# Two queue positions moved in a one-core fp32 transformer kernel: a weight split between two copies of transposed attention weights, and the memory's keys and values ahead of two splits

## The reference, cut to what matters

```python
def swiglu(h, wg, wu, wd):
    return (jax.nn.silu(h @ wg) * (h @ wu)) @ wd

def memory_cross_attention(h, mem_n, wq, wk, wv, wo, g_q, g_k):
    ...
    k = rms_norm((mem_n @ wk).reshape(B, M, MEM_HEADS, HEAD_DIM), g_k)
    v = (mem_n @ wv).reshape(B, M, MEM_HEADS, HEAD_DIM)
    ...

def attend(args):
    ...
    p = jax.nn.softmax(sc, axis=-1).astype(v_c.dtype)
    return jnp.einsum('bhqk,bkhd->bqhd', p, v_c)
```

## Time and profile before

| | us |
|---|---|
| median of 3 runs | 1170.08 (1169.73 to 1170.96) |
| the profiled execution | 1169.77 |
| its span in the profile | 1167.9 |
| busy PE / DVE / ACT / POOL | 1155.3 / 890.6 / 600.7 / 54.6 |
| granted clock of PE, mean | 1.00 |

### The profile page before, as it was taken

One profiled execution on the slowest core, in us unless ns is written; L12 is line 12 of the kernel. 1 busy time (PEld: TensorE's weight loads), 2 busy tenths in 40 slices (PEclk: granted clock), 3 DMA queues, 4 the chain that ended last, 5 costly groups with the idle time before them and its releaser, 6 DMA issues.

```text
span 1167.9 us, 15522 instructions
## 1 busy us (share of the span) xinstructions
PE 1155.3 (99%) x5969; PEld 965.9 (83%) x5969; DVE 890.6 (76%) x1598; ACT 600.7 (51%) x797; POOL 54.6 (5%) x109
## 2 busy tenths in 40 slices
PE   9999999999999999999999999999999999999998
PEld 7888888888889988888888887888898787888887
DVE  6666577987857768798886996888568777979874
ACT  7744454544445555454344464444467867545441
POOL 1100010000000000000001300000110002000000
PEclk9999999999999999999999999999999999999999
DMA  7744536555444443665453645465355142555530
GB/s 289 288 154 158 211 113 245 220 216 194 172 176 178 148 145 145 234 234 215 170 192 131 259 176 212 181 233 196 133 208 189 38 145 72 201 232 216 216 144 36
DMA packets 34689, 213.56 MB, mean 183 GB/s; under 512 B 4665, under 2 KB 6841, under 8 KB 10041
## 3 DMA queue, kind: packets, MB, share of 16 engines
q1 hardware_dynamic: 34617, 212.59, 49.0%
HBM read 211.53 MB, written 1.05 MB: 182 GB/s over the span
## 4 chain that ended last, share of the span: by engine, by line
PE 95%; DVE 2%; ACT 1%; DMA 1%; issue 1%; SPq 0%; POOL 0%; DVEq 0%; POOLq 0%
PE ps L325 30%; PE ps L326 29%; PE ps L327 29%; PE ps L331 3%; PE ps L762 1%; DVE wlo L1504 1%; DMA raw<-in_w_v 1%; PE ps L813 1%; PE ps L635 1%; PE ps L790 0%; PE ps L615 0%; DVE tmp L1523 0%; PE ps L737 0%; ACT xThi L1072 0%; PE ps L823 0%
## 5 line engine op out<-in xcount | busy, mean ns | idle before, releaser
L1504 DVE TENSOR_TENSOR wlo<-raw,whi 128x2048 fp32r<-128x2048 f32 (+2 forms) x196 | 433.1, 2232 | 45.1 <-ACT whi L1051 45.1
L1051 ACT ACTIVATE whi<-raw 128x2048 fp32r<-128x2048 f32 (+2 forms) x196 | 364.9, 1868 | 152.4 <-DMA raw<-in_w_gu 80.3
L325 PE MATMUL ps<-whi,xThi 128*128 128x512 f32 (+2 forms) x960 | 373.6, 389 | 4.3 <-issue 2.8
L327 PE MATMUL ps<-whi,xTlo 128*128 128x512 f32 (+2 forms) x960 | 371.0, 386 | 0.0
L326 PE MATMUL ps<-wlo,xThi 128*128 128x512 f32 (+2 forms) x960 | 370.8, 386 | 0.0
L325 PEld LDWEIGHTS ps<-whi,xThi 128*128 128x128 f32 x960 | 180.4, 188 | 42.9 <-issue 4.4
L327 PEld LDWEIGHTS ps<-whi,xTlo 128*128 128x128 f32 x960 | 180.4, 188 | 36.4
L326 PEld LDWEIGHTS ps<-wlo,xThi 128*128 128x128 f32 x960 | 180.5, 188 | 35.0
L1636 DVE STREAM_TRANSPOSE f_sil<-f_hid 32x128 f32<-32x128 f32 x640 | 193.8, 303 | 13.1 <-DVE f_hid L1628 0.9
L325 PE MATMUL ps<-whi,f_hThi 128*128 128x512 f32 x352 | 138.3, 393 | 0.0
L327 PE MATMUL ps<-whi,f_hTlo 128*128 128x512 f32 x352 | 137.3, 390 | 0.0
(11 more groups left out here) (289 smaller groups left out, 1160.9 us busy)
## 6 DMA issues: line engine op xcount, KB each, us to landing
raw<-in_w_gu SPq DMA_DIRECT2D x88, 1024.0 KB, 4.8
raw<-in_w_dn SPq DMA_DIRECT2D x44, 1024.0 KB, 5.2
raw<-in_w_u SPq DMA_DIRECT2D x8, 1024.0 KB, 6.3
raw<-in_w_ao SPq DMA_DIRECT2D x8, 1024.0 KB, 5.2
raw<-in_w_v SPq DMA_DIRECT2D x6, 1024.0 KB, 5.0
raw<-in_w_bv SPq DMA_DIRECT2D x4, 1024.0 KB, 4.9
raw<-in_w_bk SPq DMA_DIRECT2D x4, 1024.0 KB, 4.7
raw<-in_w_bq SPq DMA_DIRECT2D x4, 1024.0 KB, 4.9
```

Of the source, the lines that this page charges most:

```text
L325: e.matmul(ps, a[0], b[0], start=start, stop=False)
L327: return e.matmul(ps, a[1], b[0], start=False, stop=stop)
L1051: e.activation(dst[:, cs], raw_cols(i, cs), ACT.Copy).then_inc(*inc("whi", i, p))
L1504: e.tensor_tensor(lo[:, cs], raw_cols(i, cs), hi[:, cs].bitcast(F32), ALU.subtract).then_inc(*inc("wlo", i, p))
```

## The change

```diff
--- before.py
+++ after.py
@@ -1479,10 +1479,10 @@
         keys = mem_keys()
 
         def beside(c):
+            if c in (2, 3, MEM_CHUNK):
+                next(keys)
             if c == MEM_CHUNK:
                 split(2)
-            if c in (2, 3, MEM_CHUNK):
-                next(keys)
             if c == MEM_CHUNK + 4:
                 e.wait_ge(*at("clamped"))
                 a = ang[:, :, :, :].rearrange("p a b c -> p (a b c)")
@@ -1734,9 +1734,11 @@
                 weights(g)
                 if g < 3:
                     keys(g + 1, "k")
-                if g != 1:
+                if g > 1:
                     split()
                 turned_p(g, 0)
+                if g == 0:
+                    split()
                 turned_p(g, 2)
                 if g < 3:
                     keys(g + 1, "q")
```

## The result

| | us |
|---|---|
| before, median of 9 runs | 1170.08 (1169.25 to 1171.85) |
| changed, median of 9 runs | 1166.25 (1165.85 to 1167.20) |
| ratio, with its 95% interval | 0.9960 (0.9951 to 0.9968) |
| the profiled executions | 1169.77 and 1166.23 |
| their spans | 1167.9 and 1164.4 |

The change makes the kernel faster, by 0.4%. The two profiles differ by 3.54 us, where 3.47 was forecast, and the medians by 3.83. The ratio says more: 4.7 us, and the end of its interval that is nearest to 1 still says 3.7. Two questions follow.

A forecast was written before the change was run, and what follows sets the result against it. PE bounds the kernel, busy 1155.3 of 1167.9 us, leaving 12.6 us to win. Gains of 3.0 (ACT) and 0.46 (DVE), given as 3.47 us, take the median from 1170.08 to 1166.6; range 1165.8 to 1168.0.

The forecast's parts named there:

- That the gap is the copy's: Third FFN, chunk 4: PE's 2.8 us "issue" wait is for ACT's copy to `vm`, queued behind two splits.
- Its length, by starts, 3.0 us: PE's gap before unit pair 124/125, costed from matmul starts: 2.93 + 0.07 = 3.0 us gained by the ACT edit.
- the idle column: Profile's PE idle time, resting on modelled ends: 2.77 us at the `vm` gap, 3.17 us for both edits.
- the sum, 3.47: Both edits together: 3.0 us on ACT plus 0.46 us on DVE, 3.47 us gained.
- The edit on DVE, 0.46 us: Attention, head group 0: head 0's turned-weights copy steps ahead of one split, removing PE's `a_pT` wait; 0.46 us.
- Where the moved splits go: ACT's splits of units 127, 128, 129 begin at 719.4, 721.3, 723.2: later by 3.7, 2.9, 1.0 us.
- leads of 10.9 and 9.1 us: Time between DVE finishing the low halves of units 127 and 128 and PE needing them: 10.9 and 9.1 us.
- 0 for the moved splits: Delaying ACT's splits in the third FFN costs 0, covered by DVE's 7.48 us idle stretch.
- the slower rival: Low halves of units 127 and 128 miss PE's need; 6.6 us lateness falls on PE, 1173.2 us; chance 0.02.
- the step to the median: Whole kernel: profiled execution 1169.77, 0.31 under median 1170.08, becomes 1166.3, so the median becomes 1166.6 us.
- part given back: ACT's third split delays chunk 5's silu; 1.2 us of the gain is lost at later PE waits, 1167.8; chance 0.09.
- the other two: `vm` gap not due to the copy, 1169.6 us, chance 0.05; late low halves slow PE, 1173.2 us, chance 0.02.

The follow-up runs named there:

- the filled kernel: 10 unused identity matmuls added on PE where it waits for `vm`, against the kernel before; median 1170.02 us, ratio 0.9993.

## Why the prediction was right or wrong

*That the gap is the copy's*: right. It went with the ACT edit alone, grew with a third split, and once PE had work in it the profile put its name to it. *Its length, by starts, 3.0 us*: right, 2.94 from P to G (2.98 with the ACT edit alone) and the 0.07 or so of the second matmul's late start. By the Trainium skill's page "Perfetto Trace Analysis", section "Per-engine timelines", TensorE's end times are modelled. The traces agree that the starts are the better reading: 2.94 to 2.98 us went, where the idle column has 2.77. That the sum, 3.47, is so near to the 3.54 of the two profiles is in part luck, since starts of the same kernel differ by some tenths from profile to profile; and its two parts, 3.00 and 0.46, make 3.46.

*The edit on DVE, 0.46 us*: right, down to its rows (copy at 379.2, split at 379.7, next copy at 382.3, reader 0.21 behind). From the transposes to P it takes 0.46 us, from 2.64 to 2.18. In timed runs alone it is too small to be seen.

*Where the moved splits go*: right. With the 0.46 us taken off, the forecast has them from 718.9, and they began at 718.98; the silu gained a little more than forecast (724.39 against 724.6).

*"leads of 10.9 and 9.1 us", and 0 for the moved splits*: the cost was 0, the lead was wrong. 7.9 us of further delay cost 4.8; where between 0 and 7.9 it begins to cost was not measured. The step took the slack at the nearest reader. DVE's later duties, behind the normalisation of the memory's keys, have less, and lateness there was not made good within 60 us. So the slower rival's mechanism exists, and begins before the point that I gave.

*The sum*: here the prediction was wrong, for it was too small. The term that failed is that of the gap, "2.93 + 0.07 = **3.0 us**", together with the step to the median: "It would become 1166.3, and the median **1166.6 us**". Behind both stands the premise that an edit "is worth exactly what it takes out of PE's idle time": what the wait did to the clock behind it was put at nothing, without a reason. The term took what the wait cost in the one execution that was profiled, where the clock had held at 1.00. In 46 of the 60 runs of the kernel before that were timed beside the experiments the mean granted clock lies under 1.000. Two profiles show where: PE's pitch fell to that of the lower clock right behind the gap, and this cost 1.7 us in one and 2.8 in the other. With the ACT edit alone, and so without the gap, the ratio gives 4.3 us where the term says 3.0.

How much the clock is worth on average is known less well. By the runs at 1.000 against all runs beside them it is 1.3 us on one chip (1171.11 - 1169.81) and 0.9 on another (1170.99 - 1170.07); by the medians of the filled kernel 1171.25 - 1170.02 = 1.2 us, and by its ratio 0.8 (between -0.1 and 1.9). With 3.5 us this makes 4.3 to 4.8, and the ratio of the first measurement says 4.7 (between 3.7 and 5.7). The medians of that measurement were nearer to the forecast, 1166.25 for 1166.6, and this is luck: 4 of its 9 runs of the kernel before lie above 1170.5, against 46 of the 60 beside the experiments. By the ratio the changed kernel stands at 1170.08 x 0.9960 = 1165.4, under the foot of the range that was given, 1165.8.

The sign could have been had beforehand: the runs of before spread over 1.2 us with three taken, and a gap of nearly 3 us, in an engine that is idle for 12.6 us of 1167.9, was on the page. The Trainium skill, page "TensorE: Matmul & The Clock Gate", section "HAM oscillation — how this bites in real kernels", says that idleness of PE between stretches of matmuls lets its clock fall and that the matmuls behind it run slow; the prediction names this page for another rule and does not weigh this one. The traces of the later runs agree with it, for part of the executions.

*The rivals*: part given back didn't happen (G to E is 442.96 after and 443.11 before), nor did the other two in the changed kernel.

## What to carry to other kernels

When a PE-bound kernel has one gap, price it by starts, and then ask what the clock does behind it; a single profile may show the lucky case, so look at the spread of the timed runs and at a second profile. A cheap test is to fill the wait with matmuls whose result nobody uses: what it saves is the clock's part. Read the granted clock of every timed run beside its time, where it is on record. In an in-order queue put what PE waits for ahead of work that has slack, but measure that slack along the busiest helper engine and not at the first reader, and don't take "the earlier the better" for granted: here the second copy moved too far cost 0.9 us.

## What was not expected of the hardware

- The clock fell behind a wait of 2.77 us in some executions and not in others of the same kernel: two of three profiles with this gap have it (0.50 at the lowest in one, 0.70 over the stretch in the other), and of the 60 runs of the kernel before that were timed beside the experiments 46 have a mean granted clock under 1.000, with times from 1169.83 to 1172.87 us. Of the 14 runs of the changed kernel 13 have 1.000.
- It needn't fall at once. In the kernel before run against itself the first six matmuls behind the gap started 0.23 to 0.30 apart, and the pitch of 0.43 lasted from 722.5 to 725.5 only; in the DVE-only kernel it began with the first matmul and lasted 5.7 us.
- Matmuls of 128 columns of the identity kept the clock at 1.000 in 11 of 11 runs, with 0.5 us of the wait left open, and in 11 of 11 with 1.6 us left open.
